# Weight pieces with their chunks interleaved: the moving operand of the matmuls is read with a step

## The reference

```python
h = swiglu(rms_norm(x, ffn1_pre_g), gate1, up1, down1)      # 2048 -> 5632 -> 2048
x = x + 0.5 * rms_norm(h, ffn1_post_g)
u = rms_norm(x, mix_pre_g)
c_q, c_kv, k_rope, q_m, k_m, v_m = split(u @ w_in)          # 512, 256, 64, 1024, 1024, 1024
a = mla_attention(c_q, c_kv, k_rope, ...)                   # w_uq 512x1536, w_ukv 256x2048
m = moba_attention(q_m, k_m, v_m)                           # one block of 256 keys, so plain causal
y = concat[rms_norm(a, mla_out_g), rms_norm(m, moba_out_g)] @ w_out
x = x + rms_norm(y, mix_post_g)
h = swiglu(rms_norm(x, ffn2_pre_g), gate2, up2, down2)
x = x + 0.5 * rms_norm(h, ffn2_post_g)
```

## Time and profile before

| | |
|---|---|
| median of the runs | 1875.26 us |
| time of the profiled execution | 1875.26 us |
| its span, first to last instruction | 1873.4 us |
| TensorE busy (matmuls) | 1847.7 us, 99% |
| VectorE busy | 934.6 us, 50% |
| ScalarE busy | 798.7 us, 43% |
| mean granted TensorE clock | 0.997 |
| HBM traffic | 182 GB/s over the span |

### The profile page before, as it was taken

One profiled execution on the slowest core, in us unless ns is written; L12 is line 12 of the kernel. 1 busy time (PEld: TensorE's weight loads), 2 busy tenths in 40 slices (PEclk: granted clock), 3 DMA queues, 4 the chain that ended last, 5 costly groups with the idle time before them and its releaser, 6 DMA issues.

```text
span 1873.4 us, 21527 instructions
## 1 busy us (share of the span) xinstructions
PE 1847.7 (99%) x8233; PEld 1496.7 (80%) x8233; DVE 934.6 (50%) x857; ACT 798.7 (43%) x791; POOL 27.4 (1%) x59
## 2 busy tenths in 40 slices
PE   8999999999999999999999999999999999999997
PEld 6888888888878888788888878888888888788886
DVE  5444444444455554655577464444444444445545
ACT  6333433334444444543347345443333333444443
POOL 0000000000000000000000000000000000000000
PEclk9999999999999999999999999999999999999999
DMA  9454554545445545365441555555455554555552
GB/s 366 180 182 183 190 184 179 179 186 186 185 182 180 194 186 182 137 221 182 170 152 69 180 182 181 184 189 185 179 181 186 190 182 179 179 183 197 180 189 103
DMA packets 49063, 341.09 MB, mean 182 GB/s; under 512 B 5438, under 2 KB 5764, under 8 KB 9092
## 3 DMA queue, kind: packets, MB, share of 16 engines
q1 hardware_dynamic: 48944, 340.58, 50.2%
q10 hardware_dynamic: 84, 0.04, 0.0%
HBM read 338.50 MB, written 2.10 MB: 182 GB/s over the span
## 4 chain that ended last, share of the span: by engine, by line
PE 97%; DVE 1%; ACT 1%; issue 0%; DMA 0%; DVEq 0%; POOL 0%; ACTq 0%
PE banks L1191 26%; PE banks L1098 23%; PE banks L1096 23%; PE banks L1097 22%; PE banks L1161 1%; PE banks L1113 1%; DVE rows L735 0%; PE banks L1320 0%; PE banks L1321 0%; PE banks L1331 0%; DMA raw<-in_weights 0%; ACT w_hi L478 0%; DVE scaled L786 0%; PE banks L1227 0%; DVE w_lo L702 0%
## 5 line engine op out<-in xcount | busy, mean ns | idle before, releaser
L702 DVE TENSOR_TENSOR w_lo<-raw,w_hi 128x2048 fp32r<-128x2048 f32 (+3 forms) x229 | 515.1, 2249 | 671.2 <-ACT w_hi L395 671.2
L395 ACT ACTIVATE w_hi<-raw 128x2048 fp32r<-128x2048 f32 (+3 forms) x229 | 431.0, 1882 | 757.0 <-PE banks L1098 752.3
L1096 PE MATMUL banks<-w_hi,act_hi 128*128 128x512 f32 (+1 forms) x1728 | 686.1, 397 | 3.7 <-DVE act_lo L711 2.8
L1098 PE MATMUL banks<-w_hi,act_lo 128*128 128x512 f32 (+1 forms) x1728 | 683.7, 396 | 0.0
L1097 PE MATMUL banks<-w_lo,act_hi 128*128 128x512 f32 (+1 forms) x1728 | 678.4, 393 | 0.0
L1096 PEld LDWEIGHTS banks<-w_hi,act_hi 128*128 128x128 f32 x1728 | 325.4, 188 | 78.0 <-issue 3.9
L1097 PEld LDWEIGHTS banks<-w_lo,act_hi 128*128 128x128 f32 x1728 | 325.5, 188 | 77.4
L1098 PEld LDWEIGHTS banks<-w_hi,act_lo 128*128 128x128 f32 x1728 | 325.1, 188 | 77.5
L1191 PE MATMUL banks<-w_hi,hid_split 128*128 128x512 f32 x1408 | 386.1, 395 | 0.0
L775 DVE TENSOR_TENSOR w_lo<-raw,w_hi 128x2048 fp32r<-128x2048 f32 x88 | 201.6, 2291 | 236.3 <-ACT w_hi L478 236.3
L1191 PEld LDWEIGHTS banks<-w_hi,hid_split 128*128 128x128 f32 x1408 | 264.0, 188 | 65.5 <-DVE hid_split L778 0.5
(11 more groups left out here) (119 smaller groups left out, 606.5 us busy)
## 6 DMA issues: line engine op xcount, KB each, us to landing
raw<-in_weights SPq DMA_DIRECT2D x307, 1024.0 KB, 4.8
raw<-in_weights SPq DMA_DIRECT2D x6, 512.0 KB, 3.8
gain_row<-in_post_gains SPq DMA_DIRECT2D x3, 1024.0 KB, 6.9
raw<-in_weights SPq DMA_DIRECT2D x4, 768.0 KB, 4.1
raw<-in_weights SPq DMA_DIRECT2D x4, 640.0 KB, 3.8
xT<-in_x_turned SPq DMA_DIRECT2D x4, 512.0 KB, 10.2
rows<-in_x SPq DMA_DIRECT2D x2, 1024.0 KB, 13.8
out_rows<-rows SPq DMA_DIRECT2D x8, 256.0 KB, 2.8
```

Of the source, the lines that this page charges most:

```text
L395: nc.scalar.activation(w_hi[:, pc.split, 0:width], raw[:, pc.slot, 0:width], ACT.Copy)\
L702: nc.vector.tensor_tensor(w_lo[:, pc.split, 0:width], raw[:, pc.slot, 0:width], w_hi[:, pc.split, 0:width], ALU.subtract).then_inc(lo_read ...
L1096: nc.tensor.matmul(out_ap, hi, rhs_hi, start=start, stop=False, skip_group_check=chain)
L1098: return nc.tensor.matmul(out_ap, lo, rhs_hi, start=False, stop=stop, skip_group_check=chain)
```

## The change

The host lays the chunks of a piece out interleaved: column 0 of every chunk, then column 1 of every chunk. `cut` reads them so. With 4 chunks, neighbouring columns of a chunk now lie 4 floats (16 bytes) apart, with 2 chunks 2 floats (8 bytes). The size of a piece, its place in the stream and what SyncE, ScalarE and VectorE do with it are the same. Since each half of the first piece now holds columns of all four chunks, `dense_piece` waits for both halves before its first matmul.

```diff
@@ -238,7 +238,7 @@
         def cut(t, slot, chunks, width):
 
-            return t[:, slot, 0:chunks * width].rearrange("p (c n) -> p c n", c=chunks)
+            return t[:, slot, 0:chunks * width].rearrange("p (n c) -> p c n", c=chunks)
@@ -1119,6 +1119,7 @@
                 halves = isinstance(pc.index, int) and pc.index == 0
                 if halves:
                     pe.wait_ge(first_lo_ready, 1)
+                    pe.wait_ge(lo_ready, 1)
                 else:
                     pe.wait_ge(lo_ready, pc.index + 1)
@@ -1126,8 +1127,6 @@
                 for j in range(4):
                     c = 4 * i + j
-                    if halves and j == 2:
-                        pe.wait_ge(lo_ready, 1)
                     if n_turn is not None:
                         pe.wait_ge(act_ready, DC * n_turn + c + 1)
@@ -1434,7 +1433,7 @@
         groups, cols, chunks, _, width = a.shape
-        a = a.transpose(1, 0, 3, 2, 4).reshape(cols * groups, P, chunks * width)
+        a = a.transpose(1, 0, 3, 4, 2).reshape(cols * groups, P, chunks * width)
         stream[first:first + cols * groups, :, 0:chunks * width] = a
```

## The result

| | us | ratio to before, 95% interval |
|---|---|---|
| before | 1875.26 (1875.18 to 1875.34) | |
| predicted | 6130, range 2500 to 6250 | 3.27 |
| after | 3571.91 (3571.91 to 3571.92) | 1.905 (1.902 to 1.908) |

The kernel takes 1697 us longer. The direction was right, the size was not: 4255 us more had been forecast.

What follows compares the result with a forecast made beforehand. The prediction took TensorE's stream of matmuls to bound the kernel. It added 3754 us for the 16-byte step, 499 for the 8-byte step and 2.5 for the wait, +4256 on 1875.3, to reach 6130 us, range 2500 to 6250.

Steps and rivals of the forecast that it cites:

- What bounds the kernel: Whole kernel: the cost of matmuls in TensorE's stream sets the time; TensorE is busy 1847.7 of 1873.4 us.
- The 8% as the feed's limit: Contiguous matmuls: 0.4514 ns a column against 0.417, because the moving operand's feed is limited to 16 bytes every 1.81 ns.
- The step of 8 bytes: Down stages and w_ukv, 2160 matmuls: two columns from each 16-byte group, 464 ns each, +499 us.
- The step of 16 bytes: three_passes except w_ukv: one 16-byte group per column, 927 ns for each of 5280 matmuls of 512 columns, +3754 us altogether.
- The wait: First piece: TensorE waits for the second half's subtraction, starting near 10.3 us instead of 7.8; +2.5 us, between 0 and 2.5.
- A: All stepped reads: the step costs nothing and only the later start remains, 1878 us; chance 0.18.
- D: All stepped reads: they escape the contiguous read's limit, 213 ns a matmul, 149 us less, 1729 us; chance 0.02.
- B: Only the 16-byte step costs, by a factor of about two; down stages unchanged; 2925 or 3141 us, some 2500 possible; chance 0.22.
- the page rule: Moving reads: two hits on a 16-byte line absorb the access time, so 8 bytes is free and 16 bytes is not.
- C: Both steps cost a factor of two, as the feed takes words in pairs of 8 bytes; 3340 to 3650 us; chance 0.18.
- my case: All stepped reads: each 16-byte group touched costs 1.81 ns; 6130 us, by itself 5670 to 6210; chance 0.40.

Runs made afterwards that it cites:

- The forms: Three kernels without the layer, running only matmuls in many forms of the moving operand; fp32r of 512 columns: contiguous 227 ns, step of 2 floats 453, of 4 461.
- split: Kernel before, with even columns stored first, then odd ones, within each 512 (384, 320) columns of a chunk, read in turn: 1748.32 us, ratio 0.9324.
- pairs: Kernel before, with chunks interleaved in runs of two neighbouring columns and the changed kernel's wait for the first piece: 3575.71 us, ratio 1.907.

## Why the prediction was wrong

**What bounds the kernel: right.** TensorE's stream of matmuls and nothing else; the other engines kept their durations, and all 1697 us are in TensorE's busy time.

**The 8% as the feed's limit: right, and the base of all the rest.** The forms give 1.76 to 1.77 ns for a line of 16 bytes, in reads of 128, 192, 256, 320 and 512 lines, and `split`, which halves the lines each stream has to fetch, takes the excess away and 127 us with it.

**The step of 8 bytes: the number right, the reason in part.** Forecast 464 ns and +499 us, measured 453 ns and +472.5 us by itself. The 256 lines are as I counted them, but both columns of a line are not served by one fetch: each of two streams fetches all 256. That the second stream saves nothing here is luck for the forecast.

**The step of 16 bytes: the step that failed.** It read "each column needs an access of its own, at the rate at which the contiguous stream gets its groups of four, 1.81 ns a column", 927 ns and +3754 us. Each column does need a line of its own, but I took it for granted that there is one stream of lines. fp32r behaves as two, each serving every second column: 256 lines each, 460 ns, +1221.5 us (1224.4 less the 2.9 of the wait). The rows I had could not tell: a contiguous read needs all 128 lines in both streams, so one stream or two give the same 233 ns. That should have been a rival: half of my time at 16 bytes, and the same as mine at 8. By the prediction's own prices it comes to 1875 + 5280 x 0.231 + 499, about 3600 us.

**The wait: right.** +2.5 forecast, +2.9 measured, a little over the upper bound that I gave it: TensorE starts at 10.54, a quarter of a microsecond after the subtraction's end at 9.06 + 1.23 = 10.29.

**The rivals.** A (no cost) and D (faster) fell at once. B needed a free step of 8 bytes, and it costs 453 ns. It was the page rule as it stands, at least two hits on a line of 16 bytes (the Trainium skill, Advanced Engine Details and Errata, section SBUF Cachelines). The line of 16 bytes is confirmed; the two hits are not enough here: bf16 with two hits takes 452 ns and with four still 226 against 216, fp32r with two 453. C had the time (3340 to 3650), but `pairs` refutes its words of 8 bytes; that the result lies within the range of 2500 to 6250, which reached down for the sake of B and C, is luck and not a merit of my case. I held C at 0.18, with the excess as well explained by it as by mine and nothing in the rows against it, which was fair. What went wrong was to give my own case 0.40 on one inference that the rows bear out, a price for each line, followed by one that I hadn't examined, a single stream.

## What to carry to other kernels

Count the 16-byte lines that the moving operand touches, not its step: at 1.77 ns a line, a bf16 operand may leave half of each unused for 5% more (226 ns against 216), and an fp32r operand is at its limit even when contiguous. For fp32r count them for even and odd columns apart; an operand stored as all even columns, then all odd ones, and read in turn, runs within 2% of the array's own pace (216 ns against 213), and here this alone gave 6.8%. When a stream runs a few per cent slower than the array in proportion to its columns, look for such a limit before ascribing it to overhead.

## What was not expected of the hardware

- fp32r is fetched as if by two streams, even and odd columns; plain fp32 and bf16 behave as one. Plain fp32 at a step of 4 floats takes 900 ns per record instead of 429.
- The price of a line, 1.76 ns, doesn't change when the granted clock falls from 1.00 to 0.50 (bf16 at a step of 8 and of 5, 900 and 563 ns at both).
- Two regions visited in turn by one stream cost less than a fresh line each time (bf16 485 ns, not 900), and pairs in turn from two regions take 340 ns in fp32r. fp32r steps of 32 bytes and more are somewhat quicker than 16 (431 to 433 against 461 ns). No run here settles why.
- A contiguous fp32r matmul takes 227 ns in the kernels of forms and 233 in the layer. Accumulating on one bank, or changing between two operands, didn't bring the difference back (227 each). A start that moves by 1200 bytes each time gave 232 in the mean, but unevenly, 225 to 237 and at the end 260, where the layer's distances are steady. What makes the 6 ns in the layer stays open; `split` shows none of it.
